# First-layer modulation moved to TensorE, and one statistics barrier in the first transition of a hybrid encoder

## The reference

```python
cond = jax.nn.silu(c)
for i in range(DEPTH):                      # DEPTH = 2
    mod = cond @ ada_w[i] + ada_b[i]        # 1024 x 6144 weights per layer
    sh_t, sc_t, g_t, sh_c, sc_c, g_c = jnp.split(mod, 6, axis=-1)
    h = modulate(rms_norm(x, norm_g[i, 0]), sh_t, sc_t)
    h = s5_mixer(h, ...) if i == 0 else diff_attention(h, positions, ...)
    x = x + g_t[:, None, :] * rms_norm(h, norm_g[i, 1])     # residual
    h = modulate(rms_norm(x, norm_g[i, 2]), sh_c, sc_c)     # next input
    h = conv_ffn(h, ffn_w_in[i], ffn_conv_w[i], ffn_conv_b[i], ffn_w_out[i])
    x = x + g_c[:, None, :] * rms_norm(h, norm_g[i, 3])
```

## Time and profile before

| | us |
|---|---|
| median of 3 runs | 1386.8 (1385.84 to 1389.02) |
| profiled execution, whole time | 1383.9 |
| its span, first to last instruction | 1382.1 |
| PE busy | 1235.3 (89%) |
| DVE busy | 860.7 (62%) |
| ACT busy | 497.8 (36%) |
| POOL busy | 430.3 (31%) |
| mean granted TensorE clock | 0.936 of full |

### The profile page before, as it was taken

One profiled execution on the slowest core, in us unless ns is written; L12 is line 12 of the kernel. 1 busy time (PEld: TensorE's weight loads), 2 busy tenths in 40 slices (PEclk: granted clock), 3 DMA queues, 4 the chain that ended last, 5 costly groups with the idle time before them and its releaser, 6 DMA issues.

```text
span 1382.1 us, 17492 instructions
## 1 busy us (share of the span) xinstructions
PE 1235.3 (89%) x6312; PEld 994.6 (72%) x6312; DVE 860.7 (62%) x1107; ACT 497.8 (36%) x749; POOL 430.3 (31%) x274
## 2 busy tenths in 40 slices
PE   5532599988999999999999999887999999999995
PEld 0222588876888888888878776666778888887884
DVE  8999878747989744424295468775964444443323
ACT  3052342224433433414233254544544434342311
POOL 3993011123554534300020443530133344431001
PEclk9766799958999999999999999999999999999998
DMA  8001988802767513233222332220122222323211
GB/s 343 1 1 25 167 265 309 299 31 74 291 245 289 196 64 110 101 104 110 92 73 92 92 92 62 75 77 32 61 92 91 91 91 98 114 92 110 104 61 61
DMA packets 35430, 164.97 MB, mean 119 GB/s; under 512 B 4528, under 2 KB 14000, under 8 KB 17200
## 3 DMA queue, kind: packets, MB, share of 16 engines
q1 hardware_dynamic: 34368, 163.97, 35.0%
q10 hardware_dynamic: 1008, 0.27, 0.1%
HBM read 156.95 MB, written 3.08 MB: 116 GB/s over the span
## 4 chain that ended last, share of the span: by engine, by line
PE 75%; DVE 16%; issue 3%; DMA 2%; ACT 1%; SPq 1%; POOL 1%; DVEq 0%; ACTq 0%; POOLq 0%
PE psum L1738 16%; PE psum L1739 16%; PE psum L1740 16%; PE psum L1879 5%; PE psum L1880 5%; PE psum L1881 5%; PE psum L1622 2%; PE psum L1962 1%; PE psum L1937 1%; PE psum L1823 1%; SPq L375 1%; PE psum L1922 1%; PE psum L1923 1%; PE psum L1924 1%; DVE ca L1103 1%
## 5 line engine op out<-in xcount | busy, mean ns | idle before, releaser
L1738 PE MATMUL psum<-hhi,whi 128*128 128x512 f32 x960 | 382.4, 398 | 3.9 <-DVE hlo L1309 2.7
L1739 PE MATMUL psum<-hlo,whi 128*128 128x512 f32 x960 | 376.8, 393 | 0.0
L1740 PE MATMUL psum<-hhi,wlo 128*128 128x512 f32 x960 | 376.7, 392 | 0.0
L1187 DVE TENSOR_TENSOR wlo<-raw,whi 128x2048 fp32r<-128x2048 f32 x82 | 199.0, 2427 | 169.6 <-ACT whi L693 169.6
L693 ACT ACTIVATE whi<-raw 128x2048 fp32r<-128x2048 f32 x81 | 155.1, 1915 | 178.1 <-PE psum L1881 146.1
L567 POOL TENSOR_TENSOR ca<-ca,cb 128x512 f32<-128x512 f32 x44 | 138.6, 3151 | 247.2 <-ACT ca L803 247.2
L1738 PEld LDWEIGHTS psum<-hhi,whi 128*128 128x128 f32 x960 | 182.0, 190 | 45.6 <-issue 5.5
L1740 PEld LDWEIGHTS psum<-hhi,wlo 128*128 128x128 f32 x960 | 181.9, 189 | 38.6
L1739 PEld LDWEIGHTS psum<-hlo,whi 128*128 128x128 f32 x960 | 182.1, 190 | 36.2
L1403 DVE SCALAR_TENSOR_TENSOR ca<-psum,convp,ca 128x511 f32<-128x511 f32 x44 | 32.9, 749 | 200.0 <-ACT ca L799 199.9
L1879 PE MATMUL psum<-ghi,whi 128*128 128x512 f32 x352 | 137.2, 390 | 1.5 <-DVE wlo L1187 1.5
(11 more groups left out here) (344 smaller groups left out, 1736.0 us busy)
## 6 DMA issues: line engine op xcount, KB each, us to landing
raw<-in_units SPq DMA_DIRECT2D x92, 1024.0 KB, 4.8
ada_ring<-in_ada_w SPq DMA_DIRECT2D x40, 1024.0 KB, 4.8
ada_raw<-in_ada_w SPq DMA_DIRECT2D x8, 1024.0 KB, 14.9
toep<-toeplitz_rows SPq DMA_DIRECT2D x32, 128.0 KB, 8.6
qk_sw<-ca SPq DMA_DIRECT2D x32, 128.0 KB, 2.3
u<-in_x_blocks SPq DMA_DIRECT2D x1, 2048.0 KB, 14.1
x<-in_x_t SPq DMA_DIRECT2D x1, 2048.0 KB, 8.3
out_t<-x SPq DMA_DIRECT2D x8, 256.0 KB, 2.0
```

What stands on the lines that cost most here:

```text
L1187: TT(wlo[:, s, :], raw[:, s, :], whi[:, s, :].bitcast(F32), ALU.subtract).then_inc(split_lo, 1)
L1738: M(out, w_hi, hi[:, k, :], start=(k == 0), stop=False)
L1739: M(out, w_hi, lo[:, k, :], start=False, stop=False)
L1740: return M(out, w_lo, hi[:, k, :], start=False, stop=(k == KT - 1))
```

## The change

- All 24 units of layer 0's modulation (`N_ADA_PE = 3 * KT`) go through TensorE in the S5 preparation. The four products of a unit write rows 0, 32, 64 and 96 of one bank in place of row 0 of four banks. Units 8 to 23 use two slots (those of `raw`). Eight of them stand before the transposes of lb, eight between these (one after every second group). Each third's row is copied by ACT and turned by 16 products with three waits on `row_turned`.
- DVE computes the last four chunks of the modulation at the end of the output powers.
- DVE has one `ada_step` per GLU unit in place of two, and those are for layer 1; in the FFN one, two and one per unit for four units each, in place of two for twelve units.
- The first transition is a `barrier(0)` of the form of the later two, `idle_products` among it. In the GLU, ACT squares x, y and g·y and scales y by its gate; DVE adds (`tile_sums(0, i)`); POOL adds nothing there. The sum of squares of x is taken by TensorE ahead of the last GLU unit (`stat_x`).
- POOL adds seven of the eight tiles to x, in place of three.
- The first FFN unit is run as in the second FFN: half of unit 1 within unit 0, tile by tile as hlo arrives.

The diff, cut to its core:

```diff
-N_ADA_PE = KT
+N_ADA_PE = 3 * KT
...
             def load_ada0(n):
-                wait(sp, ada_used, n + 1 - N_ADA0)
+                wait(sp, ada_used, n + 1 - N_ADA0 if n < KT else n - 2 if n < KT + 2 else n - 1)
...
-            act.wait_ge(ada_used, N_ADA_PE)
-            A(mod_row[:].rearrange("p (b k) -> p b k", b=4), psum[0:1, 0:4, :], ACT.Copy).then_inc(row_copied, 1)
+            act.wait_ge(usq_added, 8)
+            copy_row(0)
             for t in range(16):
...
+                if t == 8:
+                    copy_row(1)
+            copy_row(2)
...
+            def glu_squares(f):
+                y, g = y_glu[:, f, :], gate[:, 0, f:f + 1]
+                act.wait_ge(y_ready, f + 1)
+                wait(act, sum_a, f - 2 if f > 2 else 0)
+                A(sq[:, f % 2, :] if f else ssum[:], y, ACT.Square).then_inc(sqa_ready, 1)
+                wait(act, sum_c, f - 2 if f > 2 else 0)
+                A(glu_sq[:, f % 2, :] if f else cb[:, 1, :], y, ACT.Square, scale=g).then_inc(sqc_ready, 1)
+                act.wait_ge(sqc_ready, f + 1)
+                A(y, y, ACT.Copy, scale=g).then_inc(yg_ready, 1)
...
             dve.wait_ge(row0_ready, 4)
+            dve.wait_ge(mod_psum, 2)
+            modulation(0, (2, 3, 4, 5))
+            signal(mod_read)
...
+            def glu(i, s):
+                dve.wait_ge(sig_ready, i + 1)
+                TT(y_glu[:, i, :], psum[:, 2 * s, :], ca[:, s, :], ALU.mult).then_inc(y_ready, 1)
+                if i < N_GLU - 1:
+                    split_low(i + 2, s, None)
+                    if i < KT // 2:
+                        if i:
+                            x_square_add(2 * i)
+                        x_square_add(2 * i + 1)
+                    ada_step(i, s, i // 2 + 1, i, 0)
+                tile_sums(0, i)
...
+            next_input(0, {KT - 1: lambda: second_half_low(0)})
...
-            def ada_unit(k, s):
-                pe.wait_ge(ada0_landed[s], 16 * (k // N_ADA0) + 16)
+            def ada_unit(n):
+                third, k = divmod(n, KT)
+                pe.wait_ge(ada0_landed[ada0_slot(n)], ada0_count(n))
+                if k == 0:
+                    wait(pe, row_copied, third - 1)
                 for b in range(4):
-                    ins = M(psum[0:1, b, :], cond[:, 1, k:k + 1], ada0_raw[:, s, 512 * b:512 * b + 512],
+                    ins = M(psum[32 * b:32 * b + 1, third % 2, :], cond[:, 1, k:k + 1],
+                            ada0_raw[:, ada0_slot(n), 512 * b:512 * b + 512],
                             start=(k == 0), stop=(k == KT - 1))
                 ins.then_inc(ada_used, 1)
...
+            turn_row(0)
+            for n in range(KT, 2 * KT):
+                ada_unit(n)
...
                 ins.then_inc(inb_psum, 1)
+                if t % 2:
+                    ada_unit(2 * KT + t // 2)
             pe.wait_ge(umod_rhs, 2)
             M(psum[:, 6, NB:NB + 2 * GROUPS], sel16[:].rearrange("p t c -> p (t c)"),
               ca[:, 0, 0:2 * GROUPS], start=True, stop=True).then_inc(umod_psum, 1)
+            turn_row(1)
+            turn_row(2)
...
+            pe.wait_ge(xsq_added, KT - 1)
+            for t in range(QT):
+                ins = M(psum[:, 5, t:t + 1], x_sum[:, P * t:P * t + P], col[:, 0:1],
+                        start=True, stop=True)
+            ins.then_inc(stat_x, 1)
...
-            pe.wait_ge(ada_added, 2 * N_GLU)
-            reduce_acc(0, THIRD)
-            statistic(0)
-            statistic(1)
+            barrier(0)
             ffn(0)
```

More of the change, by code:

```diff
@@ L296, in y_of @@
             return y_glu if r == 0 else y_late
[L298 to L307 removed]
+        POOL_X = 3 * (tuple(range(1, KT)),) + ((1, 3, 5),)
         def wait_x(eng, r, f):
@@ L765, in tile_squares @@
+            for i in range(N_GLU - 1):
+                glu(i, i % 2)
+            first_half_high(U_FIN[0], glu_half, 1)
+            glu(N_GLU - 1, 1)
             def tile_squares(r, f):
@@ L1398, in ffn, with body @@
                 n0, g0 = U_FIN[layer], layer * JT
-                def body(j, s, half, third=None):
+                def body(j, s, half, first=None, second=None):
                     for i, dst in enumerate((ca, cb)):
@@ L1626, in _ @@
             pe.wait_ge(cond_ready, 1)
-            for n in range(N_ADA_PE):
-                ada_unit(n, n % N_ADA0)
+            for n in range(KT):
+                ada_unit(n)
                 if n == 5:
@@ L1772, in _ @@
             glu(1, 1, 0)
-            pairs(pe, 2, N_GLU, glu)
+            pairs(pe, 2, N_GLU - 2, glu)
+            glu(N_GLU - 2, 0, None)
+            pe.wait_ge(xsq_added, KT - 1)
+            for t in range(QT):
+                ins = M(psum[:, 5, t:t + 1], x_sum[:, P * t:P * t + P], col[:, 0:1],
+                        start=True, stop=True)
+            ins.then_inc(stat_x, 1)
+            pe.wait_ge(y_ready, N_GLU - 2)
+            pe.wait_ge(split_lo, N_GLU)
+            for step in range(2 * KT):
+                ins = gemm_step(1, step, hhi, hlo)
+                if step == KT - 1:
+                    ins.then_inc(glu_half, 1)
+            ins.then_inc(unit_done, 1)
             def idle_products(n, bank):
@@ L2087, in _ada_units @@
     rows = w.reshape(2, KT, P, 3, UNIT)
-    first = rows[0, :, :, 0]
-    rest = rows[0, :, :, 1:].transpose(0, 2, 1, 3)
-    second = rows[1].transpose(2, 0, 1, 3)
-    return np.concatenate([v.reshape(-1, P, UNIT) for v in (first, rest, second)])
+    first = rows[0].transpose(2, 0, 1, 3).reshape(3 * KT, P, UNIT)
+    one, two, three = rows[1].transpose(2, 0, 1, 3)
+    both = np.stack([two[4:], three[:4]], axis=1).reshape(KT, P, UNIT)
+    return np.concatenate([first, one, two[:4], both, three[4:]])
 def _cols(v):
```

410 lines of the change are left out of this document (166 added, 244 removed).

## The result

The changed kernel took 1368.61 us (median of 4 runs, 1367.18 to 1369.6) beside 1387.45 for the kernel before: ratio 0.9863, 95% interval 0.9846 to 0.9881, 18.8 us faster. Run twice more without an edit it took 1365.72 and 1364.41 (ratios 0.9847, interval 0.9824 to 0.9869, and 0.9835, interval 0.9814 to 0.9855). Its fourteen runs lie between 1361.35 and 1369.6 with a median of 1366.45. The forecast was 1363.8, a gain of 23.0; measured gains are 18.8, 21.2 and 22.5, so it was 0.5 to 4.2 too large. The profiled execution took 1367.18 with a span of 1365.4.

What follows compares the result with a forecast made beforehand. TensorE's products set the GLU's pace; the first transition has 41.45 us without weight products. Saving 22.4 there and 0.6 from the clock, with 0 elsewhere, takes 23.0 off 1386.8: 1363.8 us, range 1360 to 1372 with rivals.

Steps and rivals of the forecast that it cites:

- The gap: First transition, last GLU product to first FFN product: 17.3 to 18.8 us, taken as 18.1, in place of 41.45.
- The tail: First transition, last GLU product to last sum on DVE: 5.3 us at least, and 5.9.
- The sum of x²: Four products on TensorE moved ahead of GLU unit 7, on TensorE's path: 0.9 us, or 1.7 at the lower clock.
- The price of a unit and of its place: S5 preparation: modulation unit 0.9 us (1.75 at lower clock), unit 8 at 48, DVE's product at 99 (95 to 109).
- Rival 1: S5 preparation: modulation units' products run two at a time, 1.75 to 3.5 us each; time 1370; chance 0.13.
- Rival 3: S5 preparation: a unit's products do not run side by side; 1378 to 1389 us, or 1432 at lower clock; chance 0.07.
- The change between transposes and units: TensorE in the S5 preparation: 16 changes of tiling, at most 0.4 us each, 6.4 in all, cost then 1.0.
- The free wait: S5 preparation: DVE's wait for TensorE's product costs nothing up to 104.4, then one us per us; cost 0 (0 to 4.6).
- GLU and kernel products keep their clock times within 1: Sign expected in the trace: GLU and kernel products start within 1 us of their earlier times.
- The clock: First FFN products behind the first transition: 31 products without a use keep TensorE active, gaining 0.6 us (0 to 1.5).
- as before, at other units: FFN: three reductions stay, only at different units; cost 0, give or take 1 us, for everything elsewhere.
- Rival 2: First transition keeps 3 to 5 us more than the later ones; time 1368; chance 0.15.

## Why the forecast was right, and where it was not

**The gap: right.** 17.3 to 18.8, taken 18.1; measured 18.57, 18.64, 18.65. The tail was 5.98, at the upper end of 5.3 to 5.9, with the waits for ACT and the modulation step in it; from the last sum on 12.6, inside 11.78 to 12.67. The sum of x² took 0.95 for 0.9. Net -22.6 + 0.9 = -21.7 on two and three traces, for -22.4.

**The price of a unit and of its place: right.** 1.04 and 1.89 (0.9, 1.75), unit 8 at 48.13 (48), product at 97.5 to 98.2 (99, 95 to 109). Rival 1, two at a time, would have had 1.75 to 3.5. Rival 3's condition, made true in the run with one column group, gave its result but for a little: 1386.7, no gain at all. Its price for that product, T = 118 up to 130, holds 126.65. That was the risk of this change, and the rows of the kernel products had already answered it.

**The change between transposes and units: its bound held and was loose.** It was bounded at 0.4 each, 6.4 in all. The run with one column group has 0.12 each, 1.9 for sixteen. In the changed kernel, with four groups, the first transpose starts 0.52 behind a unit's last record, where the next record of a unit would start 0.41 behind it: 0.11 there too, and most units wait for a load anyway. The Trainium skill, "TensorEngine Tiling (Array Packing)", Tiling Modes, has TensorE drain when the tiling mode changes. A pause of 0.1 agrees with it; that it is this drain is not shown, since the form with one group, which may not change the mode, pauses as long.

**The free wait: wrong, a small term.** The step "in sequence, the two engines' times simply add, so the wait is free up to 104.4" took POOL's time alone from what its operation costs DVE, 0.86. Alone it takes 1.12 (13.4 for twelve). A wait of 1 then saves 0.86/1.12 and costs 0.23. The runs lie on such a line, start of DVE's powers to start of what follows them: 92.67 to 128.17, 95.09 to 128.65, 97.99 to 129.36, 98.69 to 129.49, 99.54 to 129.63, that is 0.21 per us; and past POOL's end at 107.4 each us should count in full: the line has 131.3 there, 19.8 more makes 151.1, and the run with one column group, which starts at 127.18, has 150.71. So the wait to 97.5 cost 1.2 to 1.4 of DVE's time, where the sum has 0. The Trainium skill, "SBUF — State Buffer", SBUF: two separate sides, calls the ports that both share an exclusive lock and not a division of bandwidth. The trace agrees in the main: an operation of POOL costs DVE 0.86, three quarters of the 1.12 that it takes alone. A lock that cost DVE all of it would have made the wait free; the slope of 0.21 fits the remaining quarter. At the end of the preparation this 1.3 was not to be seen: without it the GLU began no earlier.

**"GLU and kernel products keep their clock times within 1": wrong, and this is the missing part.** The GLU began 3.6 later. It is not the new units, their transfers or DVE's wait (the run without them: 192.35), nor the modulation on DVE (192.91), and not chance in one trace: the third Toeplitz product stands at 173.10 and 173.21 before, and at 174.90 to 177.43 in eight traces of the changed kernel and of variants with the weights' loads in their place. All have the second Toeplitz product at 158 to 160 and then wait for the third piece's blocks. What the prediction missed is how long these transfers take, not when they start: SP begins to issue the third piece at 152.19 and 151.56 before and at 151.21 to 153.17 in the eight, and its product follows 20.9 and 21.7 later before, 23.3 to 25.1 later in the eight. The queue carries less in that time, here before and then changed:

```profile
170.00:174.00 4.00, 0.90 (x16) 0.90 (x18) 3.96 (x7) 0.00 (x0) 0.00 (x0) 0.98 1.26 129
```

```profile
170.00:174.00 4.00, 0.00 (x0) 0.00 (x0) 3.97 (x6) 0.00 (x0) 0.00 (x0) 0.50 1.22 116
```

The second trace of each has 128, and 118 and 121 in the two others of the changed kernel. Why the same transfers run slower is open; no run tried it. With the weights' loads out of their way the wait is gone (170.43).

**The clock: right in its place, too low, and given back later.** 0.6 was worked out from the first product. The run without idle products has 2.7 for its own case. Behind the transition the kernel before and the changed kernel have (first 20 us of the FFN in each, then the next 20 of the changed):

```profile
317.36:337.36 20.00, 20.00 (x81) 16.43 (x82) 14.98 (x16) 11.66 (x16) 8.35 (x5) 0.92 0.01 2
```

```profile
298.64:318.64 20.00, 20.00 (x87) 16.17 (x88) 14.82 (x22) 7.31 (x9) 5.73 (x5) 1.00 0.16 54
318.64:338.64 20.00, 20.00 (x91) 17.11 (x90) 13.14 (x9) 7.04 (x9) 12.83 (x5) 0.83 0.57 210
```

A granted clock of 0.92 over 20 us means 1.6 lost against the full one (the second trace of the kernel before: 0.90, 2.0), and all three traces of the changed kernel have 1.00 there. But the first reduction of an accumulator now stands at 320.7 instead of 384.3, and the 20 us around it have 0.83 in all three. Summed in this way over all slices of the FFN stretch, 8.6 and 7.2 are lost before and 8.4, 7.0 and 7.0 now, which goes with the stretches, 378.4 and 378.3 on average, hardly differing. The term that failed is the 0 for the reductions "as before, at other units".

**Rival 2** had 1368 and the first measurement 1368.61. Its signs are there (DVE's waits for ACT, small products at 1.84 and 1.87), but its price is refuted: the gap kept 0.5 more than taken, not 3 to 5. The number was met by luck, through the late GLU.

By terms: gap and x² 0.7 less than forecast, start of the GLU 3.6, FFN 0.4 less, the other stretches 0.2 together: 23.0 - 0.7 - 3.6 - 0.4 + 0.2 = 18.5, and the spans give 18.4. The time lies in the forecast's range because the largest term, the gap, was right; the two terms put at 0 that were not, the start of the GLU above all, make up the difference.

## What to carry to other kernels

A later place for a product that another engine waits for is not free merely because that engine's neighbour uses the pause: measure how long the neighbour's operation takes alone, not what it costs when both run. A stage whose end is set by a queue of transfers doesn't pass on what its engines gain or lose; look for what stands in that queue without need, and then for the next stop, which may be TensorE itself. And where a term is argued from two traces, check by a second trace of the same kernel how far a mark moves by itself: here 1.2 to 1.7 for the start of the GLU and 4 for the attention. When filler products or reductions are moved, sum the granted clock over the whole stage and not behind the transition alone.

## What the runs showed of the hardware

- TensorE stopped inside groups of products for 0.22 to 3.88, marked "issue", at the same two records (behind 14 of a group and behind 4 of a later one) in all three kernels whose Toeplitz blocks had landed in time, while the DMA queues were busy. In the others it waited for a transfer near that place. The DMA records of the three traces give a likely reason: a queue marked "instruction" brings one packet of 16 KB every 5 to 11 us, and each of the six stops ends 1.6 to 2.0 behind the end of such a packet (for one, packet 173.92 to 175.76, stop 173.74 to 177.63). These packets take 1.8, others of the same traces 0.9 to 1.2. So TensorE seems to have come to code that was not there yet. No edit tried it.
- Small sums (eight records) take 1.05 at the full and 1.84 to 1.87 at the lower clock; in one trace of three with the short tail they kept the full clock, and the gap was 1.2 shorter. The wait ahead of the first sum is the same in all three (1.90, 1.91, 1.90); what decided it is not shown.
- Toeplitz loads, 128 KB in packets of 512 bytes, ran at 116 to 121 GB/s in the changed kernel and 128 or 129 in the kernel before, with the engines busy (the rows from 170 to 174 above), the weights at 418 in the same queue:

```profile
158.00:162.00 4.00, 3.66 (x54) 3.32 (x56) 3.93 (x6) 0.63 (x2) 0.00 (x0) 1.00 1.01 418
```

- A change between whole-array transposes and products with one column of weights cost TensorE 0.1 to 0.12, with the products in one column group or in four.
